# A transformer stack in one kernel: paired modulation chunks, a weight split ahead of a SiLU, and value tiles, share transposes and copies in another order

## The reference

```python
# first_block, per layer (cut)
mod = silu(c) @ w_mod[i] + b_mod[i]          # six vectors of 1024: shift, scale, gate, twice
h = x * (1 + sc1) + sh1
# layer 0: 8 low-rank heads (rank 256 / 128) and 8 window heads with a sink; layer 1: difference attention
o = attention(h) @ w_out
x = layer_norm(ALPHA * x + gt1 * o)
h = x * (1 + sc2) + sh2
f = conv_ffn(h)     # silu(dwconv3(h @ w_gate) + b) * (h @ w_up), then @ w_down; 2816 hidden
x = layer_norm(ALPHA * x + gt2 * f)
```

## Time and profile before

| | |
|---|---|
| median of 3 runs | 1531.13 us |
| the profiled execution's own time | 1531.83 us |
| its span, first to last instruction | 1530.0 us |
| PE busy | 1490.3 us, 97% of the span |
| DVE busy | 851.4 us, 56% |
| ACT busy | 742.2 us, 49% |
| mean granted TensorE clock | 0.994 of full speed |

### The profile page before, as it was taken

The page is one execution under the profiler, slowest core; times in us unless marked ns, Lnnn a source line. Parts: engine busy times, 40 slices in busy tenths (PEclk is TensorE's granted clock), DMA queues, the critical chain, the costliest instruction groups (busy, mean ns, idle before and its releaser), DMA issues.

```text
span 1530.0 us, 25220 instructions
## 1 busy us (share of the span) xinstructions
PE 1490.3 (97%) x10318; PEld 1157.5 (76%) x10318; DVE 851.4 (56%) x1519; ACT 742.2 (49%) x1184; POOL 1.4 (0%) x6
## 2 busy tenths in 40 slices
PE   7999999999999999999999999999999999999986
PEld 5655567777887888789968899998998899534442
DVE  2457767744334444673597765768588875222213
ACT  3545663644223332362464764545655644555444
POOL 0000000000000000000000000000000000000000
PEclk9999999999999999999999999998999999999999
DMA  9412543243233332543226346534453357999995
GB/s 389 186 52 102 202 150 126 110 165 128 88 130 115 133 112 76 184 151 110 99 85 251 133 159 220 179 133 146 168 175 135 123 185 277 423 427 426 427 428 229
DMA packets 36374, 288.24 MB, mean 188 GB/s; under 512 B 4112, under 2 KB 4240, under 8 KB 11552
## 3 DMA queue, kind: packets, MB, share of 16 engines
q1 hardware_dynamic: 35936, 285.93, 49.6%
q0 software_dynamic: 176, 0.59, 0.1%
q10 hardware_dynamic: 144, 0.06, 0.0%
HBM read 285.51 MB, written 1.05 MB: 187 GB/s over the span
## 4 chain that ended last, share of the span: by engine, by line
PE 85%; DMA 6%; DVE 5%; ACT 2%; issue 1%; DVEq 0%; SPq 0%; ACTq 0%
PE ps L582 19%; PE ps L583 18%; PE ps L584 18%; PE ps L3239 7%; DMA deep<-wts 5%; PE ps L634 2%; PE ps L1758 1%; PE ps L1656 1%; PE ps L1729 1%; PE ps L3115 1%; PE ps L1828 1%; PE ps L1827 1%; PE ps L1826 1%; DVE WL L567 1%; PE ps L2099 1%
## 5 line engine op out<-in xcount | busy, mean ns | idle before, releaser
L582 PE MATMUL ps<-HH,WH 128*128 128x512 f32 (+2 forms) x944 | 324.8, 344 | 1.3 <-DVE WL L567 1.2
L567 DVE TENSOR_TENSOR WL<-ring,WH 128x2048 fp32r<-128x2048 f32 (+2 forms) x134 | 281.1, 2102 | 71.7 <-ACT WH L557 71.7
L583 PE MATMUL ps<-HL,WH 128*128 128x512 f32 (+2 forms) x944 | 320.4, 339 | 0.0
L584 PE MATMUL ps<-HH,WL 128*128 128x512 f32 (+2 forms) x944 | 320.1, 339 | 0.0
L557 ACT ACTIVATE WH<-ring 128x2048 fp32r<-128x2048 f32 (+2 forms) x134 | 236.1, 1764 | 123.5 <-PE ps L584 108.9
L582 PEld LDWEIGHTS ps<-HH,WH 128*128 128x128 f32 (+1 forms) x944 | 179.2, 190 | 35.1 <-issue 12.9
L584 PEld LDWEIGHTS ps<-HH,WL 128*128 128x128 f32 (+1 forms) x944 | 179.1, 190 | 20.1
L583 PEld LDWEIGHTS ps<-HL,WH 128*128 128x128 f32 (+1 forms) x944 | 179.3, 190 | 18.8 <-issue 0.2
L3239 PE MATMUL ps<-deep,arena 128*32 128x512 f32 (+1 forms) x808 | 114.9, 593 | 9.0 <-ACT other_b L3225 5.2
L582 PE MATMUL ps<-UHL,WH 128*128 128x256 f32 (+3 forms) x416 | 120.4, 289 | 0.0
L582 PE MATMUL ps<-parts,WH 128*128 128x512 f32 (+1 forms) x352 | 119.2, 339 | 0.6 <-DVE WL L567 0.6
(11 more groups left out here) (468 smaller groups left out, 2474.0 us busy)
## 6 DMA issues: line engine op xcount, KB each, us to landing
ring<-wts SPq DMA_DIRECT2D x128, 1024.0 KB, 4.9
deep<-wts SPq DMA_DIRECT2D x39, 2048.0 KB, 18.5
ring<-wts SPq DMA_DIRECT2D x32, 704.0 KB, 4.0
arena<-wts SPq DMA_DIRECT2D x13, 1024.0 KB, 12.6
under_x<-wts SPq DMA_DIRECT2D x6, 2048.0 KB, 21.6
deep<-wts SPq DMA_DIRECT2D x9, 1024.0 KB, 9.1
ring<-wts SPq DMA_DIRECT2D x4, 672.0 KB, 13.5
X<-xin SPq DMA_DIRECT2D x4, 512.0 KB, 16.3
```

The source lines that it names most:

```text
L567: e.tensor_tensor(lo, raw(i), hi.bitcast(F32), ALU.subtract).then_inc(*up("low", i))
L582: e.matmul(o, w[0][:, cols], x[0], start=k == 0, stop=False)
L583: e.matmul(o, w[0][:, cols], x[1], start=False, stop=False)
L584: return e.matmul(o, w[1][:, cols], x[0], start=False, stop=k == nk - 1)
```

## The change

1. The eight modulation chunks in the first feed-forward come in pairs, behind tiles 3, 7, 13 and 17 (`MODS_OF`); in the tile ahead of a pair DVE may make low parts of one chunk more ahead (4 entries of the plan in place of 3), and ACT looks 4 entries ahead there.
2. In the second feed-forward ACT makes the high part of the chunk of tile 3 ahead of the first SiLU, and not behind it.
3. In the attention heads two of the four value tiles are made at step 3; the share transposes stand at the start of the next step, ahead of the scores (`pe_share`), and not right behind the value product; the value product signals at its own end.
4. In steps 22 to 24 DVE turns (copies) probabilities ahead of what a modulation chunk brings with it, which in step 24 is a low part.
5. In the difference attention the first copy (of head 0) stands ahead of the maxima of head 3 (`dve_od`).

```diff
-MOD_AT = {f: 4 + i for i, f in enumerate((2, 4, 6, 8, 11, 13, 15, 17))}
+MODS_OF = {f: (4 + 2 * i, 5 + 2 * i) for i, f in enumerate((3, 7, 13, 17))}
...
-            for i in range(low_at[0], min(n + (3 if short else ahead), len(plan))):
+            for i in range(low_at[0], min(n + (4 if short else ahead), len(plan))):
...
-                    if l == 0 and f in MOD_AT:
-                        pe_mod(e, 1, MOD_AT[f])
+                    for m in MODS_OF.get(f, ()) if l == 0 else ():
+                        pe_mod(e, 1, m)
...
-                        act_high(e, c, through(l, f) if f < 2 else 3)
+                        act_high(e, c, through(l, f) if f < 2 else 4 if f in MODS_OF else 3)
...
+                    if l and f == 0:
+                        act_high(e, c, index["gu", 1, 3] + 1 - c)
                     e.wait_ge(*at("conv", l, f, 1))
                     if f >= 3:
                         e.wait_ge(*at("part_low", l, f - 3))
                     e.activation(F_.SG[:, z, :], F_.T[:, z, :], ACT.Silu).then_inc(*up("silu", l, f))
-                    if l:
-                        act_high(e, c, 4 if f else index["gu", 1, 3] + 1 - c)
+                    if l and f:
+                        act_high(e, c, 4)
...
         def pe_heads(e):
             w = weights(e, index["kvb", 0])
+            pe_value_tiles(e, w, (0, 1))
             for i in range(len(UNITS) + 3):
+                if i == 3:
+                    pe_value_tiles(e, w, (2, 3))
+                if 0 <= i - 3:
+                    pe_share(e, i - 3)
                 if i < len(UNITS):
                     pe_scores(e, i)
...
             for i in range(len(UNITS) + 4):
+                if i == 3:
+                    act_value_tiles(e, (2, 3))
                 if 0 <= i - 2 < len(UNITS):
                     act_share(e, i - 2)
...
-                if i in MODS_AT:
+                if i in MODS_AT and i <= 20:
                     dve_mod(e, 0, MODS_AT[i])
                 for j in turned_at(i):
                     dve_turn(e, j)
+                if i in MODS_AT and i > 20:
+                    dve_mod(e, 0, MODS_AT[i])
...
+        def pe_share(e, j):
+            kind, p, lat, qt = UNITS[j]
+            ot = out_tile(UNITS[j])
+            b = banks.of["o", ot, lat] if lat and qt else bank(e, "o", ot, lat)
             e.wait_ge(*at("exp.share", j))
             for q in range(query_tiles(j)):
                 c = 256 + 128 * (qt + q)
-                t = e.transpose(ps[:, b, c:c + 128], WIDE[j % 2][q], ident)
-            t.then_inc(*up("values", j))
-            if not lat or qt:
-                banks.give(b, "o_unit", ot, lat)
+                e.transpose(ps[:, b, c:c + 128], WIDE[j % 2][q], ident)
...
+                if i == 3:
+                    dve_od(e, 0)
                 if i < 8:
                     dve_diff_scores(e, i)
                 elif i == 8:
                     dve_low(e, index["dout", 0], 1)
-                e.wait_ge(*at("diff_values", i - 3))
-                e.tensor_copy(Qd[:, i - 3, :], B("od", i - 3)[:, 0:256]).then_inc(*up("od", i - 3))
+                if i > 3:
+                    dve_od(e, i - 3)
```

More of the change, by code:

```diff
@@ L215, in ffn_plan @@
                 p += [(("mod", 1, c), 2048) for c in MODS_LATE]
-            if l == 0 and f in MOD_AT:
-                p.append((("mod", 1, MOD_AT[f]), 2048))
+            if l == 0 and f in MODS_OF:
+                p += [(("mod", 1, c), 2048) for c in MODS_OF[f]]
         p += [(("down", l, half, j), HALF * 128) for j in range(8)]
@@ L1171, in act_ffn @@
                         put_off.pop(0)()
-                    if l == 0 and f in MOD_AT:
-                        act_mod(e, 1, MOD_AT[f])
+                    for m in MODS_OF.get(f, ()) if l == 0 else ():
+                        act_mod(e, 1, m)
                 act_out(e, ("down", l, half), 1, F_.tag if half else None)
@@ L1207, in dve_ffn @@
                         dve_low(e, c, 3)
-                    if l == 0 and f in MOD_AT:
-                        dve_mod(e, 1, MOD_AT[f])
+                    for m in MODS_OF.get(f, ()) if l == 0 else ():
+                        dve_mod(e, 1, m)
                     if l and f == HALF + 2:
@@ L1519, in act_prepare, with pe_value_tiles @@
                 act_keys(e, h)
-        def pe_heads(e):
-            w = weights(e, index["kvb", 0])
-            for k in range(4):
+        def pe_value_tiles(e, w, ks):
+            for k in ks:
                 b = bank(e, "vm", k)
@@ L1527, in pe_heads, with act_value_tiles @@
                 banks.give(b, "vm", k)
+        def act_value_tiles(e, ks):
+            for k in ks:
+                e.wait_ge(*at("vm_tile", k))
+                e.activation(VM[:, k, :], B("vm", k), ACT.Copy).then_inc(*up("vm", k))
+        def pe_heads(e):
+            w = weights(e, index["kvb", 0])
+            pe_value_tiles(e, w, (0, 1))
             for i in range(len(UNITS) + 3):
+                if i == 3:
+                    pe_value_tiles(e, w, (2, 3))
+                if 0 <= i - 3:
+                    pe_share(e, i - 3)
                 if i < len(UNITS):
@@ L1543, in act_heads @@
         def act_heads(e):
-            for k in range(4):
-                e.wait_ge(*at("vm_tile", k))
-                e.activation(VM[:, k, :], B("vm", k), ACT.Copy).then_inc(*up("vm", k))
+            act_value_tiles(e, (0, 1))
             act_high(e, index["qb", 0])
@@ L1749, in pe_values @@
             ot = out_tile(UNITS[j])
-            b = banks.of["o", ot, lat] if lat and qt else bank(e, "o", ot, lat)
+            b = banks.of["o", ot, lat]
             e.wait_ge(*at("p_dve", j))
             e.wait_ge(*at("p_act", j))
+            if j == 0:
+                e.wait_ge(*at("vm", 3))
             nk, nq = (4, 128) if lat else (2, 256)
@@ L1757, in pe_values @@
                     v = VM[:, vt, 64 * h:64 * h + 64] if kind == "mla" else VS[:, vt, 64 * s:64 * s + 64]
-                    e.matmul(ps[64 * s:64 * s + 64, b, 128 * qt:128 * qt + nq], v, PTA[:, j % 2, s, nq * kt:nq * kt + nq],
-                             start=kt == 0, stop=kt == nk - 1)
+                    t = e.matmul(ps[64 * s:64 * s + 64, b, 128 * qt:128 * qt + nq], v,
+                                 PTA[:, j % 2, s, nq * kt:nq * kt + nq], start=kt == 0, stop=kt == nk - 1)
+            t.then_inc(*up("values", j))
+            if not lat or qt:
+                banks.give(b, "o_unit", ot, lat)
+        def pe_share(e, j):
+            kind, p, lat, qt = UNITS[j]
+            ot = out_tile(UNITS[j])
+            b = banks.of["o", ot, lat] if lat and qt else bank(e, "o", ot, lat)
             e.wait_ge(*at("exp.share", j))
@@ L2037, in dve_diff, with dve_od @@
                                     ALU.subtract).then_inc(*up("od_low", h - 1))
+        def dve_od(e, h):
+            e.wait_ge(*at("diff_values", h))
+            e.tensor_copy(Qd[:, h, :], B("od", h)[:, 0:256]).then_inc(*up("od", h))
         def pe_diff_scores(e, j):
```

## The result

The changed kernel takes 1534.47 us in the median of 20 runs (1530.52 to 1540.55), the kernel before 1531.9 us beside it. The ratio is 1.0016, with a 95% interval of 1.0009 to 1.0022: slower by 2.6 us, where 2.5 us less were forecast, in a range that ended 0.6 us above the kernel before (1531.7 against 1531.13). The profiled execution spans 1532.4 us, with a mean granted clock of 0.995.

A forecast was written before the change was run, and what follows sets the result against it. PE, busy 97% of the span, was taken to bound the kernel. The terms −0.7 − 0.8 − 0.4 + 0.7 − 1.1 − 0.2 + 0 gave −2.5, from 1531.83 to 1529.3 us, median 1528.6; range 1525.9 to 1531.7.

The forecast's parts named there:

- The start of the heads: Scores of step 3: their 0.72 us wait for DVE's rotated keys goes, as two value tiles now lie between; −0.7 us.
- Waits inside the heads: Attention heads: PE reaches values later, so waits for probability copies shrink; waits for a bank do not; −0.4 us.
- Units with a chunk: Steps 9 to 17, nine units: the share moved from between values and chunk saves 0.09 each; −0.8 us.
- End of the heads: Last unit: shares become late, waiting for ACT's spreading behind the low part; same clock dip; next stage +0.7 us.
- the first rival: End of the heads: the clock dip does not come or falls on less work; 1.5 less, 1527.1 us; chance 0.15.
- Pairs: First feed-forward: the second chunk of a pair saves 0.27 us, loading stays hidden; four pairs, −1.1 us.
- the fifth rival: First feed-forward: the pairs starve the ring, each waiting 2.2 us, 8.8 in all; 1537.4 us; chance 0.07.
- Second feed-forward: PE's 1.25 us wait at 874.66: the low part starts at 864.2 instead of 864.33; −0.2 us.
- the fourth rival: Second feed-forward: another 1.28 us passes between table load and SiLU, low part 1.3 later; 1529.9 us; chance 0.06.
- Difference attention: PE's 0.69 us wait for DVE's copy goes, but later maxima bring another wait in its place; 0 us.
- the third: Heads: ACT and DVE pace them, 1.9 us of gains come back as waits, −0.6 stays; 1530.5 us; chance 0.20.

The follow-up runs named there:

- e7: Changed kernel with the two value tiles of step 3 behind that step's scores instead of ahead of them; 1534.07 us, ratio 1.0012.
- e5: Kernel before with the share transposes ahead of the scores alone, all four value tiles ahead of step 0; 1535.55 us, ratio 1.0018.
- e8: Changed kernel without late tiles and difference-attention copy, shares directly ahead of the values, in the last unit behind them; 1527.73 us, ratio 0.997.
- e9: As e8, but up to step 17 each share stands ahead of the scores; 1528.98 us, ratio 0.9978.
- e1: Kernel before with the pairs of modulation chunks alone; 1530.35 us, ratio 0.999.
- e4: Kernel before with the copy of the difference attention ahead of the maxima alone; 1531.29 us, ratio 0.9998.
- e6: Kernel before with two value tiles moved to step 3, ahead of the scores, alone; 1532.39 us, ratio 1.0001.
- e3: Kernel before with the attention-head edits alone: late tiles, shares ahead of scores, copies ahead of modulation in steps 22 to 24; 1534.57 us, ratio 1.0013.
- e10: As e8, but in the last unit too the shares stand ahead of the values; 1531.9 us, ratio 0.9995.
- e14: Changed kernel with two overwritten 512-column products put into the 1.5 us wait of the difference attention; 1531.9 us, ratio 0.9992.
- e2: Changed kernel with the copy of the difference attention back behind the maxima; 1533.74 us, ratio 1.0007.
- e13: The changed kernel once more, for a second profile and more runs; 1533.49 us, ratio 1.0016.
- e11: As e8, with the copy of the difference attention ahead of the maxima; 1529.97 us, ratio 0.9978.
- e12: As e8, with the last unit's sums and shares on DVE and ACT one step earlier, step 24's modulation row before ACT's high part; 1526.78 us, ratio 0.9964.

## Why the prediction was wrong

**The start of the heads is the first step that failed:** "The wait goes: −0.7", with ACT named as next late for its copies of the tiles. What was late next was a bank. I had the round of the banks in the description of the kernel and did not follow it for the moved tiles and shares: three banks taken earlier, and the scores wait for readers of unit 2. The start measured +1.46 (47.68 to 49.14) against −0.7, of which 0.9 goes with the tiles' place (e7) and 0.56 comes with the shares alone (e5). The prediction had the share at the same cost at either place in steps without a chunk, 0; of those 0.56 us, 0.29 is a wait of the queries of step 3 for ACT, in a bank that the first exponentials of unit 2 read.

**Waits inside the heads:** this term failed too. −0.4 was forecast and +0.95 measured from step 17 to 24. I weighed only what stands between turn and values, where the gain came (1.4 to 0.9). The share also stands ahead of the scores. The turn waits longer for its bank (1.2 to 1.9), and the share takes the bank of its output tile ahead of the scores, which moves the round on here as well. Followed through `Banks`, the second bank of the scores of units 18, 20, 21 and 23 was last read by the first exponentials of the unit just before; in the kernel before and in e8 it was a copy of probabilities of four units back. The scores of unit 20 wait for it, with no releaser named in the view; the exponentials in question are ACT's of unit 19, done with their sum at 193.57:

```profile
193.67 1.13 PE L1674 MATMUL ps<-arena 64*128 64x256 f32 x8 [0.32 <-issue]
...
192.79 0.69 ACT L1711 ACTIVATE arena<-ps,small 128x512 f32<-128x512 f32 x1 [1.13 <-DVE small L1698]
193.38 0.19 ACT L1711 ACTIVATION_READ_ACCUMULATOR arena<-ps,small 128x1 f32 x1
```

Back at the values, with the old round, the stretch loses 0.2 (e8); with the shares ahead of the scores only up to step 17, 0.56 (e9). How much of the 0.95 is the round and how much that the scores and all behind them start later, no run separates.

**Units with a chunk:** −0.8 forecast, −0.94 measured over the eight steps that the row of the table spans, 0.12 each. The mechanism was right and the term sized too small: values and chunk, side by side, cost nothing visible, where I had put 0.06:

```profile
149.70 1.09 PE L1776 MATMUL ps<-arena 128*64 128x128 f32 x16
150.72 1.06 PE L634 MATMUL ps<-ring,scond 128*32 128x512 f32 x8
151.72 1.09 PE L1745 MATMUL ps<-cst,arena 128*128 128x128 f32 x8
```

**End of the heads:** the mechanism was right, the shares being next late behind ACT and the low part. They start at 219.19, 7.19 us behind the chunk of step 24 (217.0 of the prediction is 7.18 behind it), after 2.21 us of wait where I had 2.7. The fall of the clock behind them, which I expected again, did not come in this execution, as the first rival had it. From the chunk of step 24 to the three chunks in a row the profile is 0.7 shorter than before, but only because before lost some 1.5 us to the clock there and this execution lost nothing; without that it is about 0.8 longer, against +0.7. The fall at this place was in all four profiles with the old end (before, e1, e4, e6), in five of the eight with the shares of the last unit ahead of its values (e3, e5, e7, e10, e14, not in changed, e2, e13) and in none of the four with them behind (e8, e9, e11, e12). The wrong part of my reading was that the cost is small: with the last shares behind the values the stretch gains (7.75 against 9.11, and 58.25 against 60.12 to the three chunks), most of it because the clock stays up.

**Pairs:** −1.1 forecast, −1.31 to −1.35 measured; the fifth rival, a ring that starves, did not come.

**Second feed-forward:** −0.2 forecast, −0.21 measured (61.87 to 61.66). The rows of the changed kernel, against the earlier trace rows:

```profile
863.38 1.90 ACT L557 ACTIVATE WH<-ring 128x2048 fp32r<-128x2048 f32 x1
865.30 1.28 ACT L1165 ACT_TABLE_LOAD   x1
866.59 0.42 ACT L1165 ACTIVATE arena<-arena 128x256 f32<-128x256 f32 x1
...
867.38 2.28 DVE L567 TENSOR_TENSOR WL<-ring,WH 128x2048 fp32r<-128x2048 f32 x1
...
877.70 0.39 PE L582 MATMUL ps<-HH,WH 128*128 128x256 f32 x1 [1.03 <-DVE WL L567]
```

The SiLU stands 1.29 behind the load's start, and the load 1.92 behind the start of a high part of 1.90: no drain shows on either side, and the fourth rival is out. The Trainium skill, "ScalarE: Activation LUTs", section "What ACT_TABLE_LOAD costs", would have put it at 2.66; this place, like the earlier trace rows, does not show it.

**Difference attention:** 0 forecast and 59.18 against 59.18 us measured at full clock. What I left out is the price of a longer wait: 0.69 became 1.46, and behind it 3 us were lost in one of five profiles.

So: +1.46 − 0.94 + 0.95 + 0.8 − 1.3 − 0.2 is +0.8 with both kernels at full clock. The kernel before, however, lost its 1.5 us at the end of the heads in every profile with that end. Against it as it ran, the end lies between −0.7 (no fall) and +2.1 (e14), and the sum between −0.7 and +2.0, unevenly from execution to execution. What is left of the measured 2.6 (1.4 to 3.4 by the interval) the copy's wait may make: the medians put e13 1.6 above e14, e11 2.2 above e8 and the changed kernel 0.7 above e2, but e4, with the copy alone, is not above the kernel before (0.9998). How much it is stays open. No rival of mine had the heads themselves slower; the third, that ACT and DVE give back the gain, came nearest and stopped at zero.

## What to carry to other kernels

Where banks or buffers are handed out in a round, moving a product changes what every later one waits for; write down who last read each bank at the moved places before pricing the move. A wait on an in-order engine belongs behind everything that does not need it: ahead of the values the last shares made the kernel about 4 us slower in the median than behind them (2.8 us at that place in the profiles), and they cost no wait at all once DVE and ACT did their sums and spreading ahead of the split. And where an edit turns a short wait into a longer one, look at the clock behind it in more than one profile before pricing it.

## What the runs showed of the hardware

Equal waits in programs alike up to there, the waits alike to 0.01 us, were followed by a granted clock of 0.5 (1.2 GHz) for 3 to 10 us in one execution and by 1.00 in another, at three places of this kernel: behind the last shares (2.21 us), behind the copy's wait, and around 1050 us, where nothing was changed (a fall of 6 to 10 us in the profiles of before, e2, e4, e6, e10, e11 and e14, a shorter one in changed, e1 and e12, none in e3, e5, e7, e8, e9 and e13). In the last 110 us too the clock fell at places that differ from profile to profile. Neither was the length of the wait the measure: 2.0 us at the scores of step 3 was followed by none in five profiles (changed, e2, e3, e13, e14), 1.9 us ahead of the last values by one in all four of the old end. With two products that fill a wait of 1.5 us at no cost in time, none of 11 runs took 1535.5 us or more, where five of 11 did without them; that the clock behind this wait is the reason is not shown.
